# A fused decoder block on one core: sink logits, one score sum and two conversions change engine or place

## The chip, the cores and the metric

The kernel runs on one core of a Trainium2 chip. The metric is the device time of one execution in microseconds (us). The engines are TensorE (PE; its weight loads are listed apart as PEld), VectorE (DVE), ScalarE (ACT), GpSimd (POOL) and SyncE (SP), which here only starts DMAs. Each engine runs its own instructions in order; semaphores order them between engines.

## The reference

528 tokens (16 learned meta tokens and 512 of the input) of width 1024 pass one decoder block:

```python
y = rmsnorm(h, mix_norm_g); z = y @ w_in
o_hg = hgrn2(...)                       # recurrence over chunks, 4 heads
# attention: 8 query heads, 2 key heads, window 128, meta tokens always visible
p = softmax(concatenate([s_band, s_meta, s_sink], -1))   # s_sink: one learned logit per head
o_at = p_band @ v_band + p_meta @ v_meta                 # the sink has no value
h = h + (g_hg * (o_hg @ w_branch_hg) + g_at * (o_at @ w_branch_attn)) @ w_out
# PEER: 8 heads x 2 key sets of 128 keys
sv, si = top_k(q . subkeys, 16)         # per head and key set
cand = sv[0][:, None] + sv[1][None, :]  # 256 pairs; top 16 of them
idx = si[0] * 128 + si[1];  g = softmax(top_s)
h = h + sum_k g * gelu(x . u[idx]) * v[idx]              # 16384 experts
out = rmsnorm(h, final_norm_g)[16:]
```

## The kernel before

Every fp32 product on TensorE is made of three: a matrix is split into a high part, which ScalarE writes with a copy (`..hi`), and a low part, the difference, which GpSimd or VectorE computes (`..lo`), and hi x hi, lo x hi and hi x lo are added in PSUM (`three`, L1490). A weight tile thus goes DMA, ScalarE, GpSimd or VectorE, TensorE, with two buffers for each part.

**Attention (about 188 to 286 us).** It begins when the recurrence ends. There are 16 head pairs of a token tile (p = 0 to 15, four to a tile; TensorE takes two heads at once). For each pair TensorE computes scores into PSUM (`scores`, semaphore `asc_mm`), VectorE's `logits` (L1135) copies the two sink logits of the pair into the column behind the keys of `atsc` (L1142), writes the scaled and masked scores beside them (L1143) and takes the negated maximum over all (L1146, `amax`); ScalarE's `exponentials` (L734) writes `atp` with its sums (`aexp`), VectorE's `normalise` divides (L1153 to L1156, `anorm`), TensorE transposes (`turn`, L1707), ScalarE copies (`turned`), TensorE multiplies with the values (`values`). Between these, TensorE computes products of the gate projection (L1573). In VectorE's program `logits(0)` is followed by `natural(3)` (L1088, L1089) and `gated(3)`, the last tile of the recurrence, whose `o_nat` TensorE transposes (L1653) before it goes on to the attention loop. In ScalarE's program the squares of that tile, one gate tile (`gate_out`: copy L694, then `split_hi` L642) and then the attention loop follow each other.

**Scores of the keys (about 386 to 487 us).** For n = 0 to 15 (a head and one of its key sets), TensorE computes queries and then scores in two halves, ScalarE copies them to `halfscore` (L848, `s_half`), GpSimd adds the halves (`score_sum`, L548, `s_out`), and VectorE finds the 16 largest (`set_tops(n)`: MAX8, FIND_INDEX8, MATCH_REPLACE8; `tops_ok`). On GpSimd the low part of the next query weights stands ahead of each sum; after the last of them come `u_split(0)`, `score_sum(14)`, `u_split(1)`, `score_sum(15)` and then `u_split(2)` and on (L558).

**Expert inputs (u tiles 0 to 127 from 482 us on).** Tile n has 24 matmuls of 352 columns, one tile being a block of 128 experts. ScalarE's loop over n < 20 holds, in this order, `top_f` at n = 2 (L886: the indices as floats, after `tops_ok` is 16), `u_split(n + 2)` (L830) and `gelu(n)` (L862). TensorE needs the low part of a tile (`u_lo`) and, since PSUM has two buffers, `gelu(n - 2)`. GpSimd makes differences of `top_f` (`step_f`) between its splits 4 to 7. Meanwhile VectorE computes `cand` (L1260), its 16 largest, softmax weights (`gate`, L1283 and L1303) and 16 `steps` tiles for each key set (L1297, L1310), which TensorE adds with identity matmuls (L1849) between u tiles, the second set ahead of tile 17.

**Expert outputs (v tiles) and the end.** Tile vb is split by ScalarE and VectorE (L1342, `v_split`; `weight_lo`, L1360) two tiles ahead of TensorE. The first token tile takes another path, through gathered rows, and ends up in `acc[:, 0]`. At vb = 124 (`FIN_AT`) ScalarE squares it and VectorE writes it to the output scaled (`scaled(0)`, L1392) right behind the low parts of v tile 126. The other three token tiles are added from PSUM (L1479), squared and scaled after the last v tile.

## Time and profile before

| | us |
|---|---|
| median of 3 runs | 1599.07 (1597.56 to 1600.12) |
| the profiled execution | 1598.55 |
| its span | 1596.8 |
| granted TensorE clock | 0.999 of full |

The profile is one execution, and its rows give start and duration of instructions; a matmul's end is modelled, so start-to-start distances are the better measure of TensorE's pace. What stands in brackets behind a row is the time for which the engine sat idle before it and what it then waited for.

### The profile page before, as it was taken

How to read it: one execution, taken by the hardware profiler on the slowest of the kernel's cores; microseconds unless marked ns; L12 is line 12 of the kernel's file. 1: busy time of each engine (PE TensorE's matmuls, PEld its weight loads, DVE VectorE, ACT ScalarE, POOL GpSimd, SP SyncE). 2: the span in 40 equal slices, each digit the busy share in tenths (PEclk: the TensorE clock that was granted, in tenths of full speed). 3: DMA queues.
4: the chain of work that ended last, by engine and by line, in shares of the span. 5: the costliest groups of instructions: out<-in, count | busy, mean ns of one | idle time of the engine just before them, and what ended most of it. 6: DMA issues, size and time to landing. Idle time of an engine off the chain costs nothing.

```text
span 1596.8 us, 25965 instructions
## 1 busy us (share of the span) xinstructions
PE 1582.3 (99%) x9610; PEld 1394.9 (87%) x9610; DVE 1256.3 (79%) x2491; ACT 691.2 (43%) x1003; POOL 735.4 (46%) x482
## 2 busy tenths in 40 slices
PE   9999999999999999999999999999999999999998
PEld 9887777778889999999999999999999999888886
DVE  5863655644889989999588888888888888888886
ACT  6223455534434457777443333333333333333334
POOL 4774344434556566665156444545444444422210
PEclk9999999999999999999999999999999999999999
DMA  4222121434223369997999999999999999888884
GB/s 154 87 92 80 54 67 54 147 117 145 80 80 119 110 210 324 305 328 253 320 349 378 345 342 339 349 338 344 343 348 340 344 342 320 294 312 309 304 320 169
DMA packets 151393, 385.42 MB, mean 241 GB/s; under 512 B 11792, under 2 KB 61200, under 8 KB 151184
## 3 DMA queue, kind: packets, MB, share of 16 engines
q1 hardware_dynamic: 59472, 203.54, 35.4%
q0 software_dynamic: 41472, 151.01, 27.0%
q10 hardware_dynamic: 50368, 29.89, 6.1%
q8 instruction: 39, 0.64, 0.2%
q14 instruction: 42, 0.34, 0.1%
HBM read 355.03 MB, written 28.84 MB: 240 GB/s over the span
## 4 chain that ended last, share of the span: by engine, by line
PE 85%; POOL 4%; issue 4%; DVE 4%; DMA 2%; ACT 1%; ACTq 0%; SPq 0%; DVEq 0%; POOLq 0%
PE ps L1490 68%; PE ps L1573 5%; PE ps L1895 4%; PE ps L1510 3%; POOL wlo L507 3%; DMA vraw<-in_v 1%; POOL score L548 1%; PE ps L1849 1%; PE ps L1707 1%; PE ps L1685 0%; PE ps L1726 0%; DMA uraw<-in_uT 0%; DVE vwlo L1342 0%; DVE mtmp L1191 0%; PE ps L1597 0%
## 5 line engine op out<-in xcount | busy, mean ns | idle before, releaser
L1490 PE MATMUL ps<-hThi,uwhi 128*128 128x352 f32 x1024 | 336.5, 329 | 2.3 <-DVE uwlo L1337 1.1
L1490 PE MATMUL ps<-hTlo,uwhi 128*128 128x352 f32 x1024 | 330.7, 323 | 0.0
L1490 PE MATMUL ps<-hThi,uwlo 128*128 128x352 f32 x1024 | 330.4, 323 | 0.0
L1490 PE MATMUL ps<-vwhi,awhi 128*128 128x512 f32 x768 | 299.5, 390 | 1.2 <-DVE awlo L1360 1.1
L1490 PE MATMUL ps<-vwlo,awhi 128*128 128x512 f32 x768 | 299.7, 390 | 0.0
L1490 PE MATMUL ps<-vwhi,awlo 128*128 128x512 f32 x768 | 299.3, 390 | 0.0
L875 ACT ACTIVATE vwhi<-vraw 128x1024 fp32r<-128x1024 f32 x128 | 135.8, 1061 | 330.2 <-PE ps L1490 294.9
L598 POOL DMA_INDIRECT rows<-in_v,gidx x128 | 147.7, 1154 | 270.2 <-DVE acc L1383 253.0
L598 POOL DMA_INDIRECT rows<-in_u,gidx x128 | 178.9, 1398 | 193.0 <-DVE rows L1376 149.3
L507 POOL TENSOR_TENSOR wlo<-raw,whi 128x1024 fp32r<-128x1024 f32 x63 | 156.0, 2476 | 222.2 <-ACT whi L642 222.1
L830 ACT ACTIVATE uwhi<-uraw 128x1024 fp32r<-128x1024 f32 x128 | 135.7, 1060 | 252.7 <-PE ps L1490 243.1
L1342 DVE TENSOR_TENSOR vwlo<-vraw,vwhi 128x1024 fp32r<-128x1024 f32 x128 | 157.1, 1227 | 104.5 <-ACT vwhi L875 104.3
L1490 PEld LDWEIGHTS ps<-hThi,uwhi 128*128 128x128 f32 x1024 | 192.1, 188 | 6.8 <-POOL uwlo L558 2.0
L1490 PEld LDWEIGHTS ps<-hTlo,uwhi 128*128 128x128 f32 x1024 | 192.7, 188 | 3.2
L1490 PEld LDWEIGHTS ps<-hThi,uwlo 128*128 128x128 f32 x1024 | 192.1, 188 | 0.0
L558 POOL TENSOR_TENSOR uwlo<-uraw,uwhi 128x1024 fp32r<-128x1024 f32 x52 | 128.7, 2475 | 94.8 <-ACT uwhi L830 94.7
L1490 PEld LDWEIGHTS ps<-vwhi,awhi 128*128 128x128 f32 x768 | 144.2, 188 | 30.9 <-DVE vwlo L1342 2.4
L1490 PEld LDWEIGHTS ps<-vwhi,awlo 128*128 128x128 f32 x768 | 144.2, 188 | 30.5
L1383 DVE SCALAR_TENSOR_TENSOR acc<-rows,pick_w,acc 128x1024 f32<-128x1024 f32 x128 | 164.2, 1283 | 4.7 <-DMA rows<-in_v,gidx 2.7
L1490 PEld LDWEIGHTS ps<-vwlo,awhi 128*128 128x128 f32 x768 | 144.1, 188 | 26.9
L1376 DVE SCALAR_TENSOR_TENSOR rows<-rows,ynat 128x1024 f32<-128x1024 f32 x128 | 155.4, 1231 | 8.3 <-DMA rows<-in_u,gidx 8.1
L1337 DVE TENSOR_TENSOR uwlo<-uraw,uwhi 128x1024 fp32r<-128x1024 f32 x76 | 92.7, 1219 | 24.8 <-ACT uwhi L830 24.8
(332 smaller groups left out, 2872.8 us busy)
## 6 DMA issues: line engine op xcount, KB each, us to landing
uraw<-in_uT SPq DMA_DIRECT2D x128, 512.0 KB, 5.3
vraw<-in_v SPq DMA_DIRECT2D x128, 512.0 KB, 5.7
raw<-in_wstream SPq DMA_DIRECT2D x70, 512.0 KB, 3.5
gmat<-gates_dram SPq DMA_DIRECT2D x64, 384.0 KB, 6.3
gates_dram<-piece ACTq DMA_DIRECT2D x11, 2048.0 KB, 13.2
xt<-in_xT SPq DMA_DIRECT2D x8, 264.0 KB, 6.0
acc<-in_x ACTq DMA_DIRECT2D x1, 2048.0 KB, 11.4
rows<-in_u,gidx POOLq DMA_INDIRECT x128, 7.1
```

Of the source, the lines that this page charges most:

```text
L507: pool.tensor_tensor(dst["lo"], raw[:, k, :], dst["hi"].bitcast(F32), ALU.subtract).then_inc(S["w_lo"], 1)
L558: pool.tensor_tensor(uw["lo"][:, n % 2, :], uraw[:, n % 2, :], uw["hi"][:, n % 2, :].bitcast(F32), ALU.subtract).then_inc(S["u_lo"], 1)
L598: pool.indirect_dma_start(out=rows[n % SLOTS][:], out_offset=None, in_=u if q < P else v, in_offset=bass.IndirectOffsetOnAxis(ap=gidx[:, q ...
L830: act.activation(uw["hi"][:, k, :], uraw[:, k, :], ACT.Copy).then_inc(S["u_hi"], 1)
L875: act.activation(vw["hi"][:, m % 2, :], vraw[:, m % 2, :], ACT.Copy).then_inc(S["v_hi"], 1)
L1337: dve.tensor_tensor(uw["lo"][:, n % 2, :], uraw[:, n % 2, :], uw["hi"][:, n % 2, :].bitcast(F32), ALU.subtract).then_inc(S["u_lo"], 1)
L1342: dve.tensor_tensor(vw["lo"][:, m % 2, :], vraw[:, m % 2, :], vw["hi"][:, m % 2, :].bitcast(F32), ALU.subtract).then_inc(S["v_lo"], 1)
L1376: dve.scalar_tensor_tensor(out=row[:], in0=row[:], scalar=1.0, in1=ynat[:, 0, :], op0=ALU.mult, op1=ALU.mult, accum_out=dots[:, k:k + 1]). ...
L1383: dve.scalar_tensor_tensor(out=acc[:, 0, :], in0=row[:], scalar=pick_w[:, k:k + 1], in1=acc[:, 0, :], op0=ALU.mult, op1=ALU.add).then_inc( ...
L1490: ins = pe.matmul(dst, lhs[a], rhs[b], start=first and i == 0, stop=last and i == 2)
L1573: ins = pe.matmul(ps[:, 2 + t % 2, :], w[a][:, t % 2, c * P:(c + 1) * P], y[b][:, c, META:LEN], start=i % (3 * DC) == 0, stop=(i + 1) % (3 ...
L1895: ins = pe.matmul(ps[:, bank, t * P:(t + 1) * P], part[:, q * 2 + t // 2, :, t % 2], hot_l[:, s, 1, q * 2 + t // 2, :, t % 2], start=i == ...
```

## The change

Five edits. (1) ScalarE writes the sink columns: `sink_column(p)` waits until its own exponentials of the pairs before p have ended (`aexp` at 2p) and then copies the two values; column 0 is written ahead of the attention loop, after waits for the sinks' DMA and for the first scores, and column i + 1 directly behind `exponentials(i)`. (2) VectorE's `logits` loses the copy and waits for `sink_ok` ahead of the maximum. (3) The sum of the score halves for n = 14 moves from GpSimd to VectorE, to the head of `set_tops(14)`; GpSimd waits for it (`s_out` at 15) ahead of `score_sum(15)`. (4) On ScalarE `top_f` moves behind `u_split(4)`, ahead of `gelu(2)`. (5) `scaled(0)` moves from vb = 124 to vb = 125, thus behind the low parts of v tile 127.

```diff
--- before.py
+++ after.py
@@ -339,7 +339,7 @@
 
 
         vec, poo = sem("vec"), sem("poo")
-        names = """g_first avm_ok akx_ok ones_ok par_in sink_in acc_in fin_in consts early_in early_in1 early_hi early_lo xsq_ok xadd_ok xsum_ok sd_ok rstd_ok z_copied gate_copied yhi_ok y_ok w_hi w_lo w_used z_out
+        names = """g_first avm_ok akx_ok ones_ok par_in sink_in sink_ok acc_in fin_in consts early_in early_in1 early_hi early_lo xsq_ok xadd_ok xsum_ok sd_ok rstd_ok z_copied gate_copied yhi_ok y_ok w_hi w_lo w_used z_out
             gate_out lb_exp lb_max f_sig og_sig hg_ok tr_mm tr_out_v tr_out_s upd_mm state_ok wsc_mm within_ok
             o_mm o_sum osd_ok on_ok ot_mm gate_sig ohg_f ohg_hi ohg_ok asc_mm amax aexp anorm atr_mm atr_out apv_mm
             oat_hi oat_ok br_f m_hi m_ok acc_mm ffn_in acc_ok ss_ok ysd_ok ynat_ok ht_mm ht_hi ht_ok q_hi q_ok s_mm s_out s_half
@@ -566,8 +566,8 @@
                                         ).then_inc(row_in[q % SLOTS], 16)
 
             u_split(0)
-            score_sum(RS - 2)
             u_split(1)
+            pool.wait_ge(S["s_out"], RS - 1)
             score_sum(RS - 1)
             for n in range(2, U_TOP + 1):
                 if n == U_TOP - 1:
@@ -747,6 +747,15 @@
                 act.activation(oat["hi"][:, :, tt * P:(tt + 1) * P],
                                ps[:, tt % 2, :].rearrange("p (c t) -> p c t", c=4), ACT.Copy).then_inc(S["oat_hi"], 1)
 
+            def sink_column(p):
+
+                need(act, S["aexp"], 2 * p)
+                act.activation(atsc[:, :, KEYS:KEYS + 1], sink[:].rearrange("p (s c) -> p s c", s=2)[:, :, p % 4:p % 4 + 1],
+                               ACT.Copy).then_inc(S["sink_ok"], 1)
+
+            act.wait_ge(S["sink_in"], 16)
+            act.wait_ge(S["asc_mm"], 1)
+            sink_column(0)
             for i in range(HEADS + 1):
                 if i >= 5 and i % 4 == 1:
                     attention_hi(i // 4 - 1)
@@ -754,6 +763,8 @@
                     turned(i - 1)
                 if i < HEADS:
                     exponentials(i)
+                if i + 1 < HEADS:
+                    sink_column(i + 1)
                 if i == HEADS:
                     attention_hi(TT - 1)
                 for t in gate_blocks_done(gates_before(i), gates_before(i + 1)):
@@ -880,10 +891,6 @@
                 act.activation(act_w["hi"][:, m % 2, :], prod[:, m % 2, :], ACT.Copy).then_inc(S["aw_hi"], 1)
 
             for n in range(U_TOP):
-                if n == 2:
-
-                    act.wait_ge(S["tops_ok"], RS)
-                    act.activation(top_f[:], top_i[:], ACT.Copy).then_inc(S["topf_ok"], 1)
                 if n == 13:
                     act.wait_ge(S["soft"], 1)
                     act.activation(gate[:], gate[:], ACT.Exp).then_inc(S["soft_exp"], 1)
@@ -901,6 +908,10 @@
                     act.activation(tab_ji[:, 0], ps[:, 7, P:TOK].rearrange("p (t k) -> p t k", k=P), ACT.Copy).then_inc(S["tj_ok"], 1)
                 if n < U_TOP - 1:
                     u_split(n + 2, n % 2)
+                    if n == 2:
+
+                        act.wait_ge(S["tops_ok"], RS)
+                        act.activation(top_f[:], top_i[:], ACT.Copy).then_inc(S["topf_ok"], 1)
                     gelu(n)
 
 
@@ -1134,15 +1145,13 @@
 
             def logits(p):
 
-                lo, c = P if p < 4 else 0, p % 4
+                lo = P if p < 4 else 0
                 dve.wait_ge(S["asc_mm"], p + 1)
-                if p == 0:
-                    dve.wait_ge(S["sink_in"], 16)
                 need(dve, S["aexp"], 2 * p)
-                dve.tensor_copy(atsc[:, :, KEYS:KEYS + 1], sink[:].rearrange("p (s c) -> p s c", s=2)[:, :, c:c + 1])
                 chain.done(dve.scalar_tensor_tensor(out=atsc[:, :, lo:KEYS], in0=ps[:, 6:8, lo:KEYS], scalar=HD ** -0.5,
                                                     in1=bandmask[:, lo:KEYS].unsqueeze(1).to_broadcast([P, 2, KEYS - lo]),
                                                     op0=ALU.mult, op1=ALU.add))
+                dve.wait_ge(S["sink_ok"], p + 1)
                 dve.tensor_reduce(atstat[:, 0, :], atsc[:, :, lo:KEYS + 1], AX_X, ALU.max,
                                   negate=True).then_inc(S["amax"], 1)
 
@@ -1226,6 +1235,10 @@
 
             def set_tops(n):
                 s = n % 2
+                if n == RS - 2:
+                    dve.wait_ge(S["s_half"], n + 1)
+                    dve.tensor_tensor(score[:, s], halfscore[:, s, :, 0, :], halfscore[:, s, :, 1, :], ALU.add
+                                      ).then_inc(S["s_out"], 1)
                 dve.wait_ge(S["s_out"], n + 1)
                 for tt in range(TT):
                     ins = dve.max(top_v[:, tt, n, 0:8], score[:, s, tt, :])
@@ -1468,7 +1481,7 @@
                     dve.wait_ge(S["dots_gelu"], c + 1)
                     dve.tensor_tensor(pick_w[:, own], dots[:, own], flat_tile(gate)[:, own], ALU.mult
                                       ).then_inc(S["dots_ok"], 1)
-                if vb == FIN_AT:
+                if vb == NK - 3:
                     scaled(0)
 
             dve.wait_ge(S["acc_back"], 16 * (TT - 1))
```

## Rows read from the trace of the kernel before

**Rows 1.** Page, part 1: busy us (share of the span) and instructions of each engine.
```profile
PE 1582.3 (99%) x9610; PEld 1394.9 (87%) x9610; DVE 1256.3 (79%) x2491; ACT 691.2 (43%) x1003; POOL 735.4 (46%) x482
```

**Rows 2.** Timeline of ScalarE, 188 to 196: start us, us, engine line operation [idle before].
```profile
189.93 1.05 ACT L642 ACTIVATE whi<-raw 128x1024 fp32r<-128x1024 f32 x1
...
195.77 0.39 ACT L742 ACTIVATE atpT<-ps 128x256 f32<-128x256 f32 x1 [2.57 <-PE ps L1708]
```

**Rows 3.** Timeline of all engines, 188 to 191, first attention pair.
```profile
188.66 0.17 DVE L1142 COPY atsc<-sink 128x2 f32<-128x2 f32 x1 [1.91 <-PE ps L1691]
...
189.22 0.45 DVE L1146 TENSOR_REDUCE atstat<-atsc 128x2 f32<-128x290 f32 x1
...
189.80 0.69 DVE L1089 TENSOR_TENSOR o_nat<-ps,o_stat 128x512 f32<-128x512 f32 x1
...
190.54 0.42 PEld L1653 LDWEIGHTS ps<-ident,o_nat 128*128 128x128 f32 x4 [0.37 <-DVE o_nat L1089]
```

**Rows 4.** Timelines of GpSimd, VectorE and TensorE, 276 to 283, last attention pair.
```profile
276.60 2.40 POOL L507 TENSOR_TENSOR wlo<-raw,whi 128x1024 fp32r<-128x1024 f32 x1 [4.02 <-ACT whi L642]
...
276.65 2.37 DVE L1142 COPY atsc<-sink 128x2 f32<-128x2 f32 x1 [1.82 <-PE ps L1685]
...
282.56 0.66 PE L1707 MATMUL ps<-ident,atp 128*128 128x128 f32 x4 [0.55 <-DVE atpm L1156]
```

**Rows 5.** Timelines of ScalarE, GpSimd and VectorE, 483 to 490, last score sums.
```profile
483.10 1.05 ACT L830 ACTIVATE uwhi<-uraw 128x1024 fp32r<-128x1024 f32 x1
...
484.54 2.39 POOL L558 TENSOR_TENSOR uwlo<-uraw,uwhi 128x1024 fp32r<-128x1024 f32 x1
...
485.17 0.28 DVE L1231 MAX8 top_v<-score 128x8 f32<-128x128 f32 x1
...
488.00 1.30 POOL L548 TENSOR_TENSOR score<-halfscore 128x512 f32<-128x512 f32 x1 [1.08 <-ACT halfscore L848]
489.25 2.39 POOL L558 TENSOR_TENSOR uwlo<-uraw,uwhi 128x1024 fp32r<-128x1024 f32 x1
```

**Rows 6.** View of line L1191: count, duration ns min/median/max, first and last start us.
```profile
L1191 DVE TENSOR_TENSOR mtmp<-mtmp x8: 691/2827/2834, 293.3 to 332.0; 128x512 f32<-128x512 f32 x8
```

**Rows 7.** Timelines of TensorE, ScalarE and GpSimd, 491 to 500, u tiles 2 to 4.
```profile
491.70 0.43 PE L1490 MATMUL ps<-hThi,uwhi 128*128 128x352 f32 x1 [0.64 <-POOL uwlo L558]
...
495.44 1.06 ACT L886 ACTIVATE top_f<-top_i 128x1024 f32<-128x1024 uint32 x1 [2.88 <-DVE top_i L1243]
...
497.53 2.39 POOL L558 TENSOR_TENSOR uwlo<-uraw,uwhi 128x1024 fp32r<-128x1024 f32 x1 [2.84 <-ACT uwhi L830]
...
499.97 0.43 PE L1490 MATMUL ps<-hThi,uwhi 128*128 128x352 f32 x1 [0.40 <-POOL uwlo L558]
```

**Rows 8.** Timelines of VectorE and TensorE, 495 to 557, index arithmetic.
```profile
495.33 2.21 DVE L1260 TENSOR_TENSOR cand<-top_v 128x512 f32<-128x512 f32 x7
...
541.21 2.91 DVE L1303 TENSOR_TENSOR gate<-gate,tot 128x512 f32<-128x512 f32 x1
544.04 9.64 DVE L1310 SCALAR_TENSOR_TENSOR steps<-ps,step_f 128x512 fp32r<-128x512 f32 x16
...
556.97 0.85 PE L1849 MATMUL ps<-steps,identr 128*128 128x512 f32 x3
```

**Rows 9.** Timelines of ScalarE, VectorE and TensorE, 1581 to 1586, last v tile.
```profile
1581.15 1.06 ACT L875 ACTIVATE vwhi<-vraw 128x1024 fp32r<-128x1024 f32 x1
...
1582.69 1.22 DVE L1342 TENSOR_TENSOR vwlo<-vraw,vwhi 128x1024 fp32r<-128x1024 f32 x1
...
1584.52 0.47 PE L1490 MATMUL ps<-vwhi,awhi 128*128 128x512 f32 x1 [0.75 <-DVE awlo L1360]
...
1585.57 2.69 DVE L1479 TENSOR_TENSOR acc<-acc,ps 128x512 f32<-128x512 f32 x4 [1.19 <-PE ps L1490]
```

**Rows 10.** Chain of work that ended last, in order of time: start us, us, what.
```profile
499.97 39.97 PE ps L1490 x240
...
549.52 7.61 PE ps L1490 x48
```

## What I expect and why

> **What bounds the kernel now.** I read the page first, then TensorE's own waits in its timeline, then the timelines of ScalarE, VectorE and GpSimd at each place that the diff touches. TensorE is busy for 1582.3 us of a span of 1596.8 us [rows 1], so 14.5 us of it are idle. Four waits of TensorE lie where the diff acts: 0.55 us before the last attention transpose [rows 4], 0.64 us before u tile 2 and 0.40 us before u tile 4 [rows 7], 0.75 us before the last v tile [rows 9]. An edit can therefore gain only where it removes one of those waits or shortens the tail, while a wait that it adds to TensorE is paid in full, because nothing later is waiting for anything but TensorE.
>
> **Sinks by ScalarE, pairs 1 to 15.** Removed: the VectorE copy of two columns in `logits`. It took 0.17 us for the first pair [rows 3], but at the last pair it took 2.37 us [rows 4]: it came 0.05 us after a GpSimd subtraction had started and ended when that one did. The subtraction of the scores (L1143) stood behind it, and all that follows it: the maximum, the exponentials, `atpm`, the transpose for which TensorE waited 0.55 us. Without the copy this chain comes some 2.3 us earlier, which is more than the wait, so the wait goes: -0.6 us with the slower restart of TensorE. The added ScalarE copies (15 of them here) are issued right behind the exponentials of the pair before, when the scores that their reader needs are not yet there. Their price is bounded above by ScalarE's 0.39 us for 256 columns and below by 0.1 us; I take 0.2, with the wait on `aexp`, at which ScalarE lets its own exponentials end. It is covered: after the exponentials of a pair ScalarE waits for the transposes, 2.57 us in the row [rows 2]. If that cover were gone it would be 15 x 0.2 = 3 us; I take 0.
>
> **Sinks by ScalarE, pair 0.** This one is not covered. It stands at the head of the attention loop, behind ScalarE's work of the last recurrence tile: `gates` copy and `split_hi`, the latter from 189.93 to 190.98 us [rows 2]. So sink 0 starts at about 190.98 and lands at about 191.2. Before, VectorE ran the maximum of pair 0 at 189.22 and `o_nat` (L1089) at 189.80, and TensorE took `o_nat` up at 190.54, with all its work before that done (its 0.37 us pause is the one it has at every such switch) [rows 3]. Now the maximum waits for `sink_ok`, and VectorE takes its instructions in order, so `natural(3)` is queued behind it: maximum at 191.2, `o_nat` at 191.2 + 0.58 = 191.78, TensorE at 191.78 + 0.74 = 192.52. That is 1.98 us later than 190.54, and TensorE has nothing else in its program: **+2.0 us**. Bounds: a ScalarE copy of 0.1 or 0.5 us gives 1.9 or 2.3; nothing gives a gain here, since ScalarE can't reach the copy before 190.98. Queued behind sink 0 on ScalarE are its table load and the exponentials of pair 0, 0.2 us later; the transposes that need them come 2 us later themselves.
>
> **One score sum on VectorE.** GpSimd loses a 1.3 us addition ahead of `u_split(1)`. That split started at 484.54; its input is ready at 483.10 + 1.05 = 484.15 [rows 5], so u tile 1 comes 0.3 us sooner. That gives TensorE nothing to keep: u tile 2 is held by `u_split(2)`, which starts at 489.25 when `score_sum(15)` ends, and that sum still stands in GpSimd's queue, started at 488.00 by ScalarE's `halfscore`. TensorE reaches tile 2 at 491.70 either way. The new wait on `s_out` ahead of that sum stands before `u_split(2)` in GpSimd's queue; it is met as long as VectorE ends its addition by 488.0. What VectorE pays: the addition has two SBUF operands and 512 columns. The one comparable addition, L1191, took 0.69 us at its fastest and 2.83 us in the median [rows 6]; the 2.1 us between are of the kind that the copy of [rows 4] lost beside a GpSimd subtraction. VectorE reaches the new one at 485.17, where the MAX8 stood [rows 5], and `u_split(1)` will run from 484.2 to 486.6. So I take the upper case: the remaining work follows the subtraction, 486.6 + 0.6 = 487.2, VectorE 2.0 us late (0.7 us if alone). 488.0 is not reached, so no loss for TensorE here: 0.
> The Trainium skill ("SBUF — State Buffer", section "SBUF: two separate sides") says that VectorE instructions with two SBUF inputs and GpSimd share one port pair as an exclusive lock, taken by whichever starts first. By that rule a GpSimd subtraction that starts second would also be held, which no row of mine shows; it speaks against this part of the change, and its result is the second rival below.
>
> **Top-k indices behind a high part.** `top_f` stood ahead of `u_split(4)` on ScalarE: it waited 2.88 us for VectorE, ran from 495.44 on for 1.06 us, the low part of tile 4 started at 497.53 and TensorE at 499.97 [rows 7]. From tile 2 at 491.70 to there are 8.27 us for 48 matmuls that take 7.61 us elsewhere [rows 10]; 0.1 us of the rest is the slower first matmul after a wait. In the new order the high part starts when TensorE is done with tile 2, about 495.9 (half way, 491.70 + 3.8, and 0.4 us for the signal), and the low part runs from 497.0 to 499.4, as tile 3 ends. I take **-0.6 us** (0.55 and the slower restart), bounds -0.4 and -0.66. `top_f` now waits for VectorE until 495.33 + 2.0 = 497.4 and ends at 498.4; queued behind it is `gelu(2)`, done by 498.9, which TensorE needs before tile 4 at 499.4. It fits by 0.5 us; `step_f` on GpSimd, behind `u_split(4)`, doesn't wait.
>
> **First token tile scaled later.** `scaled(0)` (1024 columns on VectorE, 1.2 us like the subtraction behind it) stood between the weights of the last two v tiles. The high part of the last one is ready at 1581.15 + 1.06 = 1582.21, its subtraction started at 1582.69 [rows 9]. It now starts at 1582.28, 0.41 us earlier, and so does TensorE (1584.11 for 1584.52; its own work ends 0.75 us before 1584.52). Behind it `scaled(0)` occupies VectorE until about 1585.3, so the first additions of `acc`, at 1585.57 before [rows 9], start at about 1585.28. The closing chain hangs on these: **-0.3 us**, bounds 0 and -0.4.
>
> **Sum.** +2.0 - 0.6 + 0 - 0.6 - 0.3 = +0.5 us. The profiled execution took 1598.55 us (span 1596.8), 0.52 us under the median of the runs, 1599.07. So 1599.05 for its like, and 1599.6 for the median. A difference under 0.2% (3.2 us) is about what a measurement of this kernel can't tell from none.
>
> **Rivals.**
> 1. *The sum as above*: 1599.6.
> 2. *VectorE comes too late with the steps of the second key* (slower). Being 2.0 us late, VectorE reaches the seven `cand` additions at 497.4 instead of 495.33 [rows 8], inside the subtraction of tile 4 (497.0 to 499.4). In the old trace they took 2.21 us, undisturbed. Now they end at 501 at the earliest, 4 us late, and 6.6 us late if the subtraction of tile 5 (500.8) gets in between them. Each later instruction with two SBUF operands can lose or win back some 2.2 us by where it falls, as L1303 did with 2.91 us [rows 8]. The last product of this chain, the `steps` of L1310, was issued from 544.04 on for 9.64 us, and TensorE takes it at 556.97 [rows 8]: 3.3 us to spare, 2.7 by the earlier TensorE. With VectorE 4 to 5 us late at `cand`, L1303 would find GpSimd idle and give 2.2 us back, and the wait stays at about 0. From about 6.3 us on, the next collision makes it 7.5 us and TensorE waits some 2.8 us: 1599.6 + 2.8 = 1602.4. For it: the collision at `cand` itself looks certain. Against: it takes a second one, within a few tenths.
> 3. *TensorE's pace changes.* The eight u tiles behind the wait at 499.97 ran at 39.97 / 240 = 166.5 ns a matmul, others at 7.61 / 48 = 158.5 ns, with no wait in either [rows 10]. I see no cause. If the removed wait brings the faster pace, 8 x 24 x 8.0 ns = 1.5 us go: 1598.1. Other stretches at the slow pace could follow, or the reverse.
> 4. *Pair 0 costs nothing*, because TensorE's pause at the transposes hides it or ScalarE gets there earlier: -1.5 us in all, 1597.6. The rows speak against it.
>
> **How the numbers follow.** Chances: rival 1 0.50, rival 2 0.20, rival 3 0.20, rival 4 0.10. The likeliest gives 1599.6 us. The range leaves out a tenth on each side: below, it takes in rival 4 with the lower bounds of the small terms, 1597.2; above, rival 2 with its upper part, 1602.9. Slower by over 0.2% (above 1602.3) is somewhat over half of rival 2 and a little of rival 3: 0.13. Faster by over 0.2% (under 1595.9) needs rival 3 in several stretches: 0.07. Within: 0.80.
>
> **What the new profile would show.** Right: a wait of TensorE for `o_nat` of about 2 us near 192.5; none of note before the last L1707; the wait before tile 2 larger (about 0.9 us) and none before tile 4; the last v tile's wait at 0.35 us; a VectorE addition of about 2 us near 485 (plus the shift of 2.0 - 0.6). Wrong: no wait near 190 to 193; a wait of TensorE at L1849; a GpSimd wait for `s_out` that moves tile 2; a stretch of u tiles at another pace.

## The result, and the profile after

| | before | after |
|---|---|---|
| median of 7 runs, us | 1599.07 (1597.56 to 1600.12) | 1603.93 (1601.61 to 1608.4) |
| profiled execution, us | 1598.55 | 1601.61 |
| its span, us | 1596.8 | 1599.9 |
| granted clock | 0.999 | 0.999, in its other runs 0.996 to 0.999 |

The ratio is 1.0036, with a 95% interval of 1.0027 to 1.0046: the change makes the kernel slower. That is above the forecast of 1599.6 us and above its range (1597.2 to 1602.9). The profiled execution is the fastest of the seven, and only 3.1 us above its counterpart. The median is 4.9 us above, so something costs time in other executions that this profile does not show. One execution of the kernel before beside the first four experiments took 3162.11 us and is left out of all numbers.

Line numbers have moved: L1490 is now L1503, L1653 L1666, L1707 L1720, L1260 L1273, L1297 L1310, L1303 L1316, L1310 L1323 and L1849 L1862. First the page's busy times, to be held against [rows 1]:

```profile
PE 1579.5 (99%) x9610; PEld 1392.5 (87%) x9610; DVE 1248.7 (78%) x2476; ACT 694.5 (43%) x1019; POOL 734.1 (46%) x481
```

TensorE is busy for 2.8 us less and the span is 3.1 us longer: the loss is idle time. The view of waits of TensorE says where (line, what it waited for: us in total, times, longest):

```profile
PE ps L1862 <- DVE steps L1310: 2.6, 1, 2.6
PE ps L1666 <- DVE o_nat L1100: 1.9, 1, 1.9
PE ps L1503 <- DVE uwlo L1350: 1.7, 2, 1.2
...
PE ps L1503 <- POOL uwlo L558: 1.0, 1, 1.0
```

The first two are new. The timelines of ScalarE, VectorE and TensorE from 190 to 193 us show the second, and answer [rows 2] and [rows 3]:

```profile
190.07 1.04 ACT L642 ACTIVATE whi<-raw 128x1024 fp32r<-128x1024 f32 x1
191.02 0.19 ACT L753 ACTIVATE atsc<-sink 128x2 f32<-128x2 f32 x1
...
191.32 0.46 DVE L1155 TENSOR_REDUCE atstat<-atsc 128x2 f32<-128x290 f32 x1 [2.03 <-ACT atsc L753]
...
191.89 0.69 DVE L1100 TENSOR_TENSOR o_nat<-ps,o_stat 128x512 f32<-128x512 f32 x1
...
192.64 0.66 PE L1666 MATMUL ps<-ident,o_nat 128*128 128x128 f32 x4 [1.89 <-DVE o_nat L1100]
```

ScalarE's first sink copy comes behind `split_hi`. VectorE's maximum waits for it, `o_nat` stands behind the maximum, and TensorE starts at 192.64, 2.10 us later than at 190.54.

The timelines of GpSimd, VectorE, ScalarE and TensorE from 485 to 504 us answer [rows 5], [rows 7] and the first line of [rows 8]:

```profile
485.57 2.38 POOL L558 TENSOR_TENSOR uwlo<-uraw,uwhi 128x1024 fp32r<-128x1024 f32 x1 [3.69 <-ACT uwhi L841]
...
498.40 2.41 POOL L558 TENSOR_TENSOR uwlo<-uraw,uwhi 128x1024 fp32r<-128x1024 f32 x1 [2.69 <-ACT uwhi L841]
500.73 0.79 POOL L586 COPY step_f<-top_f 128x64 f32<-128x64 f32 x1
502.20 2.45 POOL L558 TENSOR_TENSOR uwlo<-uraw,uwhi 128x1024 fp32r<-128x1024 f32 x1 [0.68 <-ACT uwhi L841]
...
486.52 1.99 DVE L1240 TENSOR_TENSOR score<-halfscore 128x512 f32<-128x512 f32 x1
...
498.71 7.29 DVE L1273 TENSOR_TENSOR cand<-top_v 128x512 f32<-128x512 f32 x7
...
498.83 1.07 ACT L914 ACTIVATE top_f<-top_i 128x1024 f32<-128x1024 uint32 x1 [0.51 <-DVE top_i L1256]
...
493.09 0.43 PE L1503 MATMUL ps<-hThi,uwhi 128*128 128x352 f32 x1 [1.00 <-POOL uwlo L558]
```

The moved sum takes 1.99 us. The seven additions of `cand` start 0.31 us behind a GpSimd subtraction and take 7.29 us instead of 2.21. One by one, the first took 2.65 us and ended 0.55 us behind that subtraction, and the sixth took 2.54 us, beside the subtraction of 502.20. The seventh took 1.21 us instead of 0.41, beside the next GpSimd instruction (L589, from 504.62 on); the other four were nearly as short as before. The wait before tile 2 has grown from 0.64 to 1.00 us, and before tile 4 there is none now.

Then the timelines of VectorE and TensorE from 538 to 550 us, and the end of the kernel ([rows 8] and [rows 9] of before):

```profile
538.96 9.65 DVE L1310 SCALAR_TENSOR_TENSOR steps<-ps,step_f 128x512 fp32r<-128x512 f32 x16
...
549.63 0.69 DVE L1316 TENSOR_TENSOR gate<-gate,tot 128x512 f32<-128x512 f32 x1
...
548.67 3.98 PE L1862 MATMUL ps<-steps,identr 128*128 128x512 f32 x16 [2.60 <-DVE steps L1310]
...
1587.49 0.47 PE L1503 MATMUL ps<-vwhi,awhi 128*128 128x512 f32 x1 [0.31 <-DVE awlo L1373]
```

The first 16 `steps` tiles start on VectorE 8.4 us later than the 530.55 us of before, and TensorE waits 2.60 us for the last of them.

The distance between the two traces at matched matmuls, after minus before, goes as follows: +2.10 us at `o_nat` (192.64 for 190.54), +1.44 behind the last attention pair, +1.03 in u tile 1, +1.39 at tile 2 (493.09 for 491.70), +0.89 at tile 4, +0.25 just before the steps, +3.02 at the steps (548.67 for 545.65), about +4 in the middle of the u tiles, +2.97 at the last v tile (1587.49 for 1584.52), and +3.1 in the span.

### The profile page after: what moved, and what is told of

It is laid out like the page before. It is cut to its first block, busy times and chain, and to the rows that moved or that the text cites. A ratio compares the mean times of both kernels' runs of the same rounds, so it can differ in the third digit from the quotient of the medians.

```text
span 1599.9 us, 25981 instructions
## 1 busy us (share of the span) xinstructions
PE 1579.5 (99%) x9610; PEld 1392.5 (87%) x9610; DVE 1248.7 (78%) x2476; ACT 694.5 (43%) x1019; POOL 734.1 (46%) x481
## 4 chain that ended last, share of the span: by engine, by line
PE 83%; DVE 6%; POOL 4%; issue 4%; ACT 1%; DMA 1%; ACTq 0%; SPq 0%; DVEq 0%; POOLq 0%
PE ps L1503 66%; PE ps L1586 6%; PE ps L1908 4%; POOL wlo L507 3%; PE ps L1523 2%; POOL score L548 1%; DVE steps L1310 1%; PE ps L1720 1%; PE ps L1698 0%; PE ps L1862 0%; DVE cand L1273 0%; PE ps L1739 0%; DMA vraw<-in_v 0%; DMA uraw<-in_uT 0%; DVE pos_u L1291 0%
## 5 line engine op out<-in xcount | busy, mean ns | idle before, releaser
L1503 PE MATMUL ps<-hThi,uwhi 128*128 128x352 f32 x1024 | 336.3, 328 | 2.7 <-DVE uwlo L1350 1.7
L1503 PE MATMUL ps<-hTlo,uwhi 128*128 128x352 f32 x1024 | 330.5, 323 | 0.0
L1503 PE MATMUL ps<-hThi,uwlo 128*128 128x352 f32 x1024 | 330.3, 323 | 0.0
L1503 PE MATMUL ps<-vwhi,awhi 128*128 128x512 f32 x768 | 299.3, 390 | 0.7 <-DVE awlo L1373 0.7
L1503 PE MATMUL ps<-vwlo,awhi 128*128 128x512 f32 x768 | 299.6, 390 | 0.0
L1503 PE MATMUL ps<-vwhi,awlo 128*128 128x512 f32 x768 | 299.3, 390 | 0.0
L598 POOL DMA_INDIRECT rows<-in_u,gidx x128 | 180.7, 1412 | 192.6 <-DVE rows L1389 147.6
L1503 PEld LDWEIGHTS ps<-hThi,uwhi 128*128 128x128 f32 x1024 | 192.1, 188 | 7.1 <-DVE uwlo L1350 2.2
L1503 PEld LDWEIGHTS ps<-hTlo,uwhi 128*128 128x128 f32 x1024 | 192.7, 188 | 3.2
L1503 PEld LDWEIGHTS ps<-hThi,uwlo 128*128 128x128 f32 x1024 | 192.1, 188 | 0.0
L558 POOL TENSOR_TENSOR uwlo<-uraw,uwhi 128x1024 fp32r<-128x1024 f32 x52 | 128.9, 2478 | 101.0 <-ACT uwhi L841 100.9
L1503 PEld LDWEIGHTS ps<-vwhi,awlo 128*128 128x128 f32 x768 | 144.2, 188 | 30.3
L1503 PEld LDWEIGHTS ps<-vwhi,awhi 128*128 128x128 f32 x768 | 144.2, 188 | 29.5 <-DVE vwlo L1355 1.5
L1503 PEld LDWEIGHTS ps<-vwlo,awhi 128*128 128x128 f32 x768 | 144.1, 188 | 27.3
```

The source lines that it names most:

```text
L558: pool.tensor_tensor(uw["lo"][:, n % 2, :], uraw[:, n % 2, :], uw["hi"][:, n % 2, :].bitcast(F32), ALU.subtract).then_inc(S["u_lo"], 1)
L598: pool.indirect_dma_start(out=rows[n % SLOTS][:], out_offset=None, in_=u if q < P else v, in_offset=bass.IndirectOffsetOnAxis(ap=gidx[:, q ...
L1503: ins = pe.matmul(dst, lhs[a], rhs[b], start=first and i == 0, stop=last and i == 2)
```

## The experiments

Each was timed beside the kernel before on the same chip, so ratios can be compared across the groups and medians only within one. That kernel's median was 1598.3 us beside the first four, 1599.23 beside the next four and 1598.15 beside the last two. "Clock" is the granted clock of the profiled execution. No run takes edit 5, or edit 1 for the pairs 1 to 15, back by itself; what they give is read from the traces.

| run | what it is | median us (range, runs) | ratio (95%) | span, clock |
|---|---|---|---|---|
| e0_changed_again | the change | 1604.06 (1601.95 to 1604.81, 5) | 1.0035 (1.0021 to 1.0048) | 1602.3, 0.997 |
| e1_sink0_vector | sink 0 back on VectorE | 1600.73 (1598.82 to 1601.7, 11) | 1.0012 (1.0003 to 1.0021) | 1599.0, 0.999 |
| e2_sum_gpsimd | score sum back on GpSimd | 1599.79 (1597.74 to 1601.77, 11) | 1.0010 (1.0001 to 1.0019) | 1598.7, 0.998 |
| e3_both_undone | both back | 1596.89 (1595.71 to 1598.07, 11) | 0.9992 (0.9983 to 1.0001) | 1595.4, 0.999 |
| e4_only_sum | before, and the moved sum alone | 1602.45 (1599.57 to 1604.62, 11) | 1.0020 (1.0011 to 1.0029) | 1601.6, 0.998 |
| e5_sum_from_psum | e1, the sum reads PSUM | 1598.14 (1597.03 to 1598.63, 11) | 0.9993 (0.9984 to 1.0003) | 1596.6, 0.999 |
| e6_sink0_ahead | e2, sink 0 earlier on ScalarE | 1598.12 (1596.93 to 1598.96, 11) | 0.9993 (0.9984 to 1.0002) | 1597.2, 0.999 |
| e7_sink0_behind | e2, sink 0 later still | 1603.3 (1601.83 to 1604.16, 8) | 1.0022 (1.0012 to 1.0033) | 1601.1, 0.997 |
| e8_both_repaired | e5 and e6 in one | 1598.51 (1597.5 to 1601.44, 11) | 1.0003 (0.9994 to 1.0012) | 1596.6, 0.999 |
| e9_both_undone_again | e3 once more | 1597.19 (1595.36 to 1600.2, 11) | 0.9993 (0.9984 to 1.0002) | 1597.5, 0.998 |

### The change once more: e0

No edit; a second profile, since the first was its kernel's fastest run.

> The changed kernel once more, beside the kernel before on the same chip. Its profile stands 3.1 us over before's in the span, but its median 4.9 us over, and its runs spread over 6.8 us where before's spread over 2.6. Theory W (waits): TensorE's new waits at the last recurrence tile (1.9 us) and at the index steps (2.6 us) are all there is, and the median is about 3 us over before. Theory C (clock): on top of the waits, TensorE's granted clock falls for some us in some executions; then executions of this kernel show a mean clock of 0.998 or less where before shows 0.999, and each 0.001 goes with some 1.6 us.

The windows view of e0 (stretch, its length, busy us and count of PE, PEld, DVE, ACT, POOL, then granted clock, DMA share, GB/s):

```profile
190.00:192.70 2.70, 0.82 (x4) 0.33 (x4) 1.23 (x3) 2.67 (x5) 1.58 (x1) 1.00 0.00 0
192.70:196.20 3.50, 3.50 (x12) 2.82 (x13) 1.65 (x5) 0.86 (x5) 2.01 (x2) 0.53 0.39 123
196.20:200.00 3.80, 3.80 (x24) 3.00 (x23) 0.91 (x2) 0.65 (x3) 0.00 (x0) 0.98 0.06 25
```

A stretch of nearly the same time in the kernel before:

```profile
193.00:196.40 3.40, 3.40 (x23) 2.63 (x22) 2.81 (x7) 0.78 (x5) 1.71 (x2) 1.00 0.49 146
```

TensorE waits 1.88 us for `o_nat`, and directly behind the wait its clock is half (1.2 GHz) for some 3.4 us: 12 matmuls where before has 23. Matmuls of 512 columns start 0.43 us apart (194.02, 194.45, 194.88) and, once the clock is back, 0.23 us apart (196.48, 196.71). The Trainium skill ("TensorE: Matmul & The Clock Gate", Part 1) gives 426.7 ns for 512 columns at 1.2 GHz, and these rows agree with it. Against the kernel before, the lag (the distance at matched matmuls) grows from 2.02 us at the wait to 3.58 us twelve matmuls on: the wait costs another 1.6 us. The same happens behind the 2.42 us wait for the steps, where the lag grows from 5.01 to 6.68 us. The first profile of the change had both waits and neither fall. So both profiles have the waits, and only one has the falls behind them. A fall of 3.4 us to half lowers the mean clock by 3.4 x 0.5 / 1600 = 0.001, so by this estimate the runs at 0.998 had one such fall, those at 0.997 two, and the one at 0.996 three or longer ones.

The twelve executions of the change (7 and these 5) bear this out: three with a clock of 0.999 took 1602.5 us in the mean, four at 0.998 took 1603.5, four at 0.997 took 1605.2, and one at 0.996 took 1608.4. The clock is not all of the spread: the median run of the result, 1603.93 us, had 0.999. Expected were waits alone (theory W, 3 us) or waits and clock (theory C); the 5.8 us and the falls speak for C.

### Each costly part taken back: e1, e2, e3

```diff
# e1: sink 0 on VectorE, as before
-            act.wait_ge(S["sink_in"], 16)
-            act.wait_ge(S["asc_mm"], 1)
-            sink_column(0)
...
+                if p == 0:
+                    dve.wait_ge(S["sink_in"], 16)
+                    dve.tensor_copy(atsc[:, :, KEYS:KEYS + 1], sink[:].rearrange("p (s c) -> p s c", s=2)[:, :, 0:1])
...
-                dve.wait_ge(S["sink_ok"], p + 1)
+                need(dve, S["sink_ok"], p)
# e2: score sum 14 on GpSimd, between u_split(0) and u_split(1)
+            score_sum(RS - 2)
             u_split(1)
-            pool.wait_ge(S["s_out"], RS - 1)
...
-                if n == RS - 2:
-                    dve.wait_ge(S["s_half"], n + 1)
-                    dve.tensor_tensor(score[:, s], halfscore[:, s, :, 0, :], halfscore[:, s, :, 1, :], ALU.add
-                                      ).then_inc(S["s_out"], 1)
```

> The changed kernel, with the sink column of pair 0 written by VectorE again; columns 1 to 15 stay with ScalarE. Theory W: the wait of TensorE for o_nat (1.89 us near 192.6) goes, and 1.9 us with it; the wait at the index steps stays at about 2.6 us. Theory C1 (the clock falls because of this wait): besides, the spread and the clock return to those of before, so 3 to 4 us less in the median. Theory C2 (it falls because of the wait at the index steps): the spread stays and the median loses only 1.9 us.

> The changed kernel with the score sum of n = 14 on GpSimd again. If VectorE's lateness is what makes TensorE wait at the index steps, VectorE reaches the cand additions 3.4 us sooner than in the changed kernel (by the 1.99 us of the sum and what it displaces), they don't take 7.3 us, and the wait of 2.6 us goes: 2.6 us less. Rival: the moved top_f alone, by which GpSimd's subtraction of u tile 4 starts earlier, into the cand additions, makes them late, and at least half of the wait stays. C2 would give the clock back too.

> The changed kernel with both undone: what is left is ScalarE's sinks for pairs 1 to 15, top_f behind the high part, the later scaling. By the sum of the prediction without its cost: -0.6 - 0.6 - 0.3 = -1.5 us against before, within the noise of one chip but a wait of TensorE less at the last attention pair, at u tile 4 and at the last v tile. Under theory W its clock and spread are those of before; if they are not, neither of the two waits is what disturbs the clock.

VectorE's seven additions in e1, in e2 and in e3:

```profile
497.42 7.28 DVE L1273 TENSOR_TENSOR cand<-top_v 128x512 f32<-128x512 f32 x7
```

```profile
498.52 2.22 DVE L1269 TENSOR_TENSOR cand<-top_v 128x512 f32<-128x512 f32 x7
```

```profile
494.52 2.22 DVE L1269 TENSOR_TENSOR cand<-top_v 128x512 f32<-128x512 f32 x7
```

In e1 GpSimd's subtraction of tile 4 had started at 497.09, 0.33 us ahead of them: 7.28 us, and TensorE waits 2.60 us for the steps. In e2 and e3 the additions start 1.7 us ahead of the subtraction (500.21, 496.22): 2.22 us and no wait for the steps. Their last ones hold that subtraction, which takes 2.78 us instead of 2.40, and TensorE waits 0.26 us before tile 4. So without the moved sum neither the later `top_f` nor the late first pair makes the additions late, and the rival of e2's expectation is out. In e2 the wait for `o_nat` stays at 1.9 us, with a half-clock stretch of 3.4 us behind it, and 8 of its 11 runs have a clock of 0.998 or less; e1 keeps the wait for the steps and has 0.998 in 7 of 11. So the clock falls behind either wait, and neither C1 nor C2 is right alone. In e3 both waits are gone and the clock is 0.999 in all.

From e3 (1596.89) the first sink adds 2.9 us (e2), the moved sum 3.8 us (e1), both together 7.2 us (e0). The waits are 1.9 and 2.6 us. The rest goes largely with the clock: the runs of e2 and e1 with a clock of 0.999 or more stand 1.8 and 2.9 us above e3 in the mean, those with less 3.5 and 4.0 us. e3 stands 1.4 us under before, where 1.5 was expected.

### The moved sum alone: e4

```diff
             u_split(0)
-            score_sum(RS - 2)
             u_split(1)
+            pool.wait_ge(S["s_out"], RS - 1)
             score_sum(RS - 1)
...
+                if n == RS - 2:
+                    dve.wait_ge(S["s_half"], n + 1)
+                    dve.tensor_tensor(score[:, s], halfscore[:, s, :, 0, :], halfscore[:, s, :, 1, :], ALU.add
+                                      ).then_inc(S["s_out"], 1)
```

> The kernel before with one edit, the score sum of n = 14 on VectorE; top_f stays ahead of the high part of u tile 4. The sum should take about 2.0 us beside GpSimd's subtraction, as it does in the changed kernel, and VectorE's top-16 end 2.0 us later. Theory P (what made the seven cand additions take 7.3 us is that top_f's new place lets GpSimd subtract tile 4 just then): here top_f comes 2.0 us later and holds tile 4 back, TensorE waits 2.4 us there instead of 0.4, cand runs before the subtraction in 2.2 us, and no wait is left at the index steps: +2.0 us against before. Rival: cand is stretched here too and TensorE waits in both places, +4 us or more.

Timelines of VectorE, GpSimd and TensorE in e4:

```profile
485.45 1.99 DVE L1231 TENSOR_TENSOR score<-halfscore 128x512 f32<-128x512 f32 x1
...
497.65 2.22 DVE L1264 TENSOR_TENSOR cand<-top_v 128x512 f32<-128x512 f32 x7
...
499.85 2.36 POOL L558 TENSOR_TENSOR uwlo<-uraw,uwhi 128x1024 fp32r<-128x1024 f32 x1 [5.00 <-ACT uwhi L830]
...
502.26 0.66 PE L1494 MATMUL ps<-hThi,uwhi 128*128 128x352 f32 x1 [2.37 <-POOL uwlo L558]
```

Here `top_f` still stands ahead of the high part of tile 4. VectorE's lateness goes through it to GpSimd's split, and TensorE waits 2.37 us at tile 4, where it waited 0.40 [rows 7], with half the clock from 502.2 to 505.6 us. The additions escape the collision, because the split is late too. Edit 4 of the change takes away this wait and puts the additions beside the subtraction: the price moves from tile 4 to the steps. So the collision takes both edits, the moved sum and the moved `top_f`. Theory P holds in its order of events; its +2.0 us was too low. The sum alone costs 3.2 us (1602.45 for 1599.23), and the trace shows where the rest lies: the lag grows by another 1.4 us in the half-clock stretch (2.29 to 3.72 us).

### The moved sum without the shared port: e5

```diff
-                    dve.tensor_tensor(score[:, s], halfscore[:, s, :, 0, :], halfscore[:, s, :, 1, :], ALU.add
+                    there = ps[:, 2:4, :].rearrange("p b (t a n) -> p (b t) a n", t=2, a=2)
+                    dve.tensor_tensor(score[:, s], there[:, :, 0, :], halfscore[:, s, :, 1, :], ALU.add
```

> The changed kernel with sink 0 on VectorE (as in e1), and the score sum still on VectorE but with its first operand read from PSUM, where the same numbers lie, so that only one operand is in SBUF. If it is two SBUF operands that make a VectorE instruction wait for GpSimd, it takes 0.7 us instead of 1.99, VectorE comes 1.3 us sooner to cand, part of cand still meets the subtraction of tile 4 (up to 2.6 us), and TensorE's wait at the index steps goes: about 3 us less than e1, the level of e3 (1597). Rival: any SBUF operand is enough; then it takes 1.99 us as before and the time is that of e1 (1600.7).

Timelines of VectorE, GpSimd and TensorE in e5:

```profile
485.04 0.68 DVE L1241 TENSOR_TENSOR score<-ps,halfscore 128x512 f32<-128x512 f32 x1
...
495.93 2.22 DVE L1274 TENSOR_TENSOR cand<-top_v 128x512 f32<-128x512 f32 x7
...
496.93 3.46 POOL L558 TENSOR_TENSOR uwlo<-uraw,uwhi 128x1024 fp32r<-128x1024 f32 x1 [2.68 <-ACT uwhi L838]
...
500.44 0.43 PE L1504 MATMUL ps<-hThi,uwhi 128*128 128x352 f32 x1 [0.95 <-POOL uwlo L558]
```

The addition now takes 0.68 us with a GpSimd subtraction beside it (484.09 to 486.49), where the SBUF form took 1.99. VectorE reaches `cand` at 495.93, ahead of the subtraction of tile 4, and is not held. GpSimd is: its subtraction takes 3.46 us where 2.40 is normal, ends 1.1 us late, and TensorE waits 0.95 us at tile 4. The stretched `cand` that was expected did not come; the same lock was paid by the other engine. The ratio stands 0.0019 (3.0 us) under that of e1, as expected. The rival, that any SBUF operand is enough to be held, is out for this addition, which still reads one. It doesn't follow that only two SBUF operands are held: the sink copy of [rows 4] has one, and took 2.37 us.

### The first sink earlier and later: e6, e7

```diff
# e6: in the loop over the tiles of the recurrence; its old place is gone
+                if tt == TT - 1:
+                    act.wait_ge(S["sink_in"], 16)
+                    act.wait_ge(S["asc_mm"], 1)
+                    sink_column(0)
                 for t in gate_blocks_done(
...
-            act.wait_ge(S["sink_in"], 16)
-            act.wait_ge(S["asc_mm"], 1)
-            sink_column(0)
             for i in range(HEADS + 1):
# e7: three copies of 2 x 272 columns ahead of sink_column(0)
+            for k in range(3):
+                act.activation(atp[:, :, 0:KEYS], bandmask[:].unsqueeze(1).to_broadcast([P, 2, KEYS]), ACT.Copy).then_inc(S["filled"], 1)
+                act.wait_ge(S["filled"], k + 1)
             sink_column(0)
```

> e2 (score sum on GpSimd) with sink 0 still written by ScalarE, but ahead of the last gate tile's copy and high part instead of behind them, at about 189.7 us. If the wait for o_nat comes from the place in ScalarE's queue, it falls from 1.9 us to 0.4 to 0.7 us. Theory C (a long wait of TensorE is what lets its clock fall): at that length the clock doesn't fall in the following stretch, so 1.3 us less from the wait and up to another 1 us in the median of e2, 1599.8: about 1597.7, clock 0.999. Rival (the clock falls at any new wait here): 1598.5 and clocks of 0.998.

> The other way: e2 with three extra copies on ScalarE (544 columns each, into a buffer not in use) ahead of sink 0, so that TensorE's wait for o_nat grows from 1.9 us by about 2.1 to some 4 us. By the wait alone +2.1 us against e2 (1599.8), 1601.9. Theory C: the clock falls behind it in nearly every execution, where e2 shows it in most but not all; then clocks of 0.998 or lower throughout and 1602 to 1603.5, with the stretch behind the wait at half clock for some 3 us in the profile.

ScalarE's copy and TensorE's restart in e6, then in e7:

```profile
189.57 0.19 ACT L715 ACTIVATE atsc<-sink 128x2 f32<-128x2 f32 x1
...
191.19 0.66 PE L1663 MATMUL ps<-ident,o_nat 128*128 128x128 f32 x4 [0.45 <-DVE o_nat L1101]
```

```profile
190.64 2.02 ACT L759 ACTIVATE atp<-bandmask 128x544 f32<-128x544 f32 x3
192.69 0.21 ACT L753 ACTIVATE atsc<-sink 128x2 f32<-128x2 f32 x1
...
194.33 0.90 PE L1665 MATMUL ps<-ident,o_nat 128*128 128x128 f32 x3 [3.95 <-DVE o_nat L1103]
```

The copy at 189.57, 191.02 and 192.69 us gives a wait for `o_nat` of 0.45, 1.89 and 3.95 us: TensorE follows this copy, wherever it stands. In e6 the clock is 0.999 or more in all 11 runs, as expected, where e2 has 8 of 11 at 0.998 or less. In e7 it is 0.998 or less in all 8. There the clock is at half for 6.8 us from 192.6 us on, 5.1 us of them behind the restart, and the lag against before grows in them from 3.78 to 6.11 us: 2.3 us for this longer fall, 1.6 in e2. In the times, e7's wait is 2.1 us longer than e2's and its ratio stands 0.0012 (1.9 us) higher, though the two intervals overlap; they can't resolve the 0.7 us between the falls.

### Both repairs, and e3 again: e8, e9

Edits: e5's addition and e6's place of the sink in one kernel; and e3 unchanged.

> The changed kernel with both repairs at once: sink 0 put in by ScalarE ahead of its gate tile, and score sum 14 on VectorE with its first operand from PSUM. The earlier runs give the repair of sink 0 a wait of 0.45 us for o_nat and the sum from PSUM 0.68 us on VectorE, with no wait of TensorE for the steps. If the two costs are separate and there is nothing else in the change that costs, this kernel keeps both small: wait for o_nat about 0.45 us, a wait of up to 1 us before u tile 4 (GpSimd held by the seven additions), none at the steps, a clock of 0.999, and a median near those of its two halves, 1598.1 us: ratio 0.999 to 1.0000. If the two interact (VectorE being 0.5 us late moves the seven additions back into a GpSimd subtraction), the additions take 4 to 7 us, the wait for the steps comes back and the median lies near 1600.

> The changed kernel without its two costly parts (column 0 by VectorE, score sum 14 on GpSimd), the same kernel as e3, once more on another chip. It keeps sinks of pairs 1 to 15 (-0.64), the later conversion (-0.5) and the later scaling (-0.3 to -0.4), so by the sum of the traces it should stand 1.4 to 1.5 us under the kernel before: ratio 0.9991. If the 0.9992 of its first series was chance and the removed waits give nothing, the ratio is 1.0000 or above.

e8 did as its first case says: wait for `o_nat` 0.45 us, before tile 4 0.9 us, none for the steps, `cand` 2.22 us, clock 0.999. Its ratio, 1.0003, is a little above what was expected and can't be told from 1. So with both prices cut down, the change is worth nothing measurable: what its good parts give, the rest of its two bad ones takes.

e9 gives 0.9993 after 0.9992. Taken together, the two intervals of +-0.0009 make 0.99925 +-0.00064 (0.0009 over the root of 2), just under 1: a gain of about 1.2 us where the traces foretell 1.5. No kernel here has a lower ratio, but e5 and e6, at 0.9993, can't be told from it, and it is less than the 0.2% that the prediction asked of a difference.

e9's profile shows the fall of the clock in a place that no edit touches. Its timeline of TensorE at a u tile near 774 us:

```profile
773.84 0.43 PE L1499 MATMUL ps<-hThi,uwhi 128*128 128x352 f32 x1 [2.63 <-DVE uwlo L1346]
...
775.78 0.49 PE L1499 MATMUL ps<-hThi,uwhi 128*128 128x352 f32 x1
776.07 0.49 PE L1499 MATMUL ps<-hTlo,uwhi 128*128 128x352 f32 x1
...
778.73 0.32 PE L1499 MATMUL ps<-hThi,uwlo 128*128 128x352 f32 x1
```

The wait is 2.63 us here and 0.70 us before; from 1.1 us behind the restart, matmuls of 352 columns start 0.29 us apart instead of 0.16, for 3.4 us. The chain behind the wait leads to ScalarE, whose high part stands behind the instruction that starts the DMA of `gates_dram` (L936 here). That took 4.23 us, against 2.29 in before, 2.00 in e3, 2.76 in e5 and 3.04 in e8, where TensorE waited 0.70, 0.41, 1.18 and 1.45 us: always 1.6 us less. So the same program, e3 and e9, differs by 2.2 us at this one place. The three slowest runs of e9 (1600.2, 1599.22, which is this one, and 1598.05 us) are the three with a clock of 0.998.

## Why the prediction was wrong

**Pair 0, +2.0: right.** The wait is 1.89 us, `o_nat` starts at 191.89 (191.78 was worked out), TensorE at 192.64 (192.52). e6 and e7 show the chain by moving its first link. (The 0.37 us pause was not "the one it has at every such switch": the three earlier switches of before, at 165.53, 175.37 and 185.21 us, have none. It was already a wait for `o_nat`, which is why any lateness of it is paid in full.)

**Pairs 1 to 15, -0.6: right.** No wait is left before the last transpose; the lag shrinks by 0.63 us there.

**Score sum, size right, consequence wrong.** The addition took 1.99 us beside GpSimd, and VectorE was 2.1 us late at `cand` in e1 (497.42 for 495.33), as forecast. In the changed kernel it was 3.4 us late (498.71), since the whole kernel ran 1.4 us later. The sentence that failed is "so no loss for TensorE here: 0", together with rival 2's "it takes a second one, within a few tenths". The prediction saw the collision at `cand` as certain and set its price at 4 us if one subtraction lay in it, 6.6 if a second got between ("501 at the earliest" is 3.5 us behind the 497.54 of before; its 4 us mean 501.5). The second one did, in every profile of the changed order (7.29, 7.28 and 6.67 us in after, e1 and e0): 5.1 us of stretch on top of the 2.1 in e1, and TensorE waited 2.60 us where the sum has 0. The prediction's own numbers spoke for it: additions that end at 501.5 reach into a subtraction that starts at 500.8. In time the moved sum cost 3.8 us (e1 over e3).

**The slack was taken at the wrong steps.** The prediction worked out the second set ([rows 8], TensorE at 556.97) and let L1303 win back 2.2 us before it. That did happen (L1316 took 0.69 us, at 549.63), and it helps only the second set. The first set ends ahead of it: 530.55 + 9.65 = 540.20 us for TensorE at 545.65, 5.45 us to spare. VectorE is 8.41 us late there and TensorE 0.25: 8.41 - 5.45 - 0.25 = 2.71 us, and the wait measured is 2.60. So the threshold lay at 5.45 us plus TensorE's own lateness, at the first steps: 5.7 us in the profiled run, and 4.5 in e1, where TensorE was 1.0 us early. It was not 6.3 us at the second steps, and the lateness of 7.2 us in e1 was well past it. Rival 2's price of 2.8 us was right, for another reason than the one given; its chance of 0.20 was the error.

**The clock, not in the sum.** A wait was priced at its own length. Behind the waits of 1.9 to 2.6 us the clock fell to half in some of the executions, and each fall cost 1.4 to 1.7 us more (e0; also e2, e4 and e9), the longer one of e7 2.3 us. With this, the change costs 2.0 + 2.6 for its waits, -1.5 for what it gains and up to 3.2 for two falls: 3.1 to 6.3 us; the profiled execution is at the lower end (+3.1) and the median of the runs (+4.9, in e0 +5.8) toward the upper. A clock of 0.998 or less was seen in 5 of 7 and 4 of 5 runs of the change, 7 of 11 of e1, 8 of 11 of e2 and e4 each and 8 of 8 of e7, which all have a wait of 1.9 us or more in the places of the edits. Without such a wait it was seen in none of 44 runs of e3, e5, e6 and e8, in 3 of 11 of e9, and in 5 of 77 of the kernel before beside the experiments.

**Top-k indices, -0.6: right in size (-0.5), with a condition.** The wait at tile 4 is gone. The prediction's order of events (`top_f` from 497.4 to 498.4) came out at 498.83 to 499.90, without a wait of TensorE. What it did not say is that this move brings the subtraction of tile 4 forward, onto the additions: with `top_f` in front (e4) they aren't touched.

**First token tile, -0.3: right.** TensorE's wait at the last v tile is 0.31 us (0.35 was forecast); from the last matmul to the end it takes 0.1 us longer.

**Rival 3, the pace.** From tile 4 on, 240 matmuls (ten tiles; the prediction says eight) take 39.17 us in after and 39.8 in before, start to start. Tile by tile the mean is 159 to 163 or 166 to 167 ns, and once per trace about 171, in an order that changes from trace to trace, with the same program too: 39.17 us in e3 and 39.56 in e9. e5 and e8, where TensorE waits 0.9 us before tile 4, take 39.37 and 39.38. So nothing ties the pace to the removed wait; the difference is worth 0.6 us here, and its cause stays open.

**The lock.** No row of the prediction showed GpSimd held by VectorE, but the trace of before does: a subtraction of L558 that started at 631.26, 0.48 us behind a two-operand VectorE instruction (L1367, 630.78), took 3.01 us instead of 2.40, and six more of L558 took 2.7 or 3.0 us. By the Trainium skill ("SBUF — State Buffer", section "SBUF: two separate sides") whichever starts first holds the port pair; e5's 3.46 us for a subtraction that started inside the additions agrees, and so do the 2.78 us of e2 and e3.

## What to carry to other kernels

Before moving work to an engine with spare time, follow its lateness down to every point where the critical engine takes something from it, the first one above all, and compare it with the slack there; slack that is won back later doesn't help the first taker. A two-SBUF-operand instruction on VectorE beside a GpSimd stream is a matter of order to a few tenths of a microsecond: reading one operand from PSUM took the moved sum out of that (0.68 us), though not the additions behind it. And a new wait of TensorE of about 2 us should be priced at 2 us plus a half-clock stretch behind it, here 1.6 us, in part of the executions.

## What the runs showed of the hardware

- TensorE's clock fell to half behind waits as short as 1.88 us (e0), 1.9 (e2), 2.37 (e4), 2.42 (e0) and 2.63 us (e9), and did not behind 1.89 and 2.60 us in the profiled run of the change and 2.60 us in e1's: the length of the wait alone does not decide it. What does was not found. Behind waits of up to 1.45 us (e8) no profile shows a fall while matmuls follow. Each fall began between 0.1 us before the restart (e4) and 1.1 us behind it (e9), in e7 1.7 us before it.
- Seven additions on VectorE, back to back, held a GpSimd subtraction for 1.06 us (3.46 for 2.40 in e5), yet once they stood behind a subtraction, a second one got in between them (6.67 to 7.29 us for 2.21).
- A 128 x 512 addition on VectorE beside a GpSimd subtraction took 1.99 us with both operands in SBUF and 0.68 us with one in PSUM.
- One instruction of ScalarE that starts a DMA (`gates_dram`) took 2.00 us in e3 and 4.23 us in e9, the same program; TensorE's wait behind it was 0.41 and 2.63 us.
